# First overflow tile of a mixture-of-experts stage as a conditional 17th expert, without the barriers around it

## The reference, cut to what matters

```python
def moe(x, router_w, router_bias, w_gate, w_up, w_down):
    scores = sigmoid(x @ router_w)
    ...
    gate = take_along_axis(scores, idx, axis=-1)
    gate = gate / gate.sum(-1, keepdims=True)
    w = (one_hot(idx, N_EXPERTS) * gate[..., None]).sum(1)
    hg = einsum('nd,edf->nef', x, w_gate)
    hu = einsum('nd,edf->nef', x, w_up)
    hh = silu(hg) * hu * w[:, :, None]
    return einsum('nef,efd->nd', hh, w_down)

def trunk(...):
    for l in range(2):
        y, st = mixer_block(x, ...)
        x = layer_norm(ALPHA * x + y, ln1_g[l], ln1_b[l])
        x = layer_norm(ALPHA * x + moe(x, ...), ln2_g[l], ln2_b[l])
```

## Time and profile before

| what | value |
|---|---|
| median of 3 runs | 1659.1 us (1656.07 to 1663.48) |
| profiled execution, its own time | 1656.69 us |
| its span, first to last instruction | 1654.9 us |
| busy, share of the span | PE 1379.6 us (83%), PEld 892.5 us (54%), DVE 698.6 us (42%), ACT 440.1 us (27%), POOL 126.9 us (8%) |
| mean granted TensorE clock | 0.915 of full speed |
| HBM traffic | 187.48 MB read, 31.83 MB written, 133 GB/s over the span |

### The profile page before, as it was taken

The page is one execution under the profiler, slowest core; times in us unless marked ns, Lnnn a source line. Parts: engine busy times, 40 slices in busy tenths (PEclk is TensorE's granted clock), DMA queues, the critical chain, the costliest instruction groups (busy, mean ns, idle before and its releaser), DMA issues.

```text
span 1654.9 us, 19434 instructions
## 1 busy us (share of the span) xinstructions
PE 1379.6 (83%) x7575; PEld 892.5 (54%) x7575; DVE 698.6 (42%) x1381; ACT 440.1 (27%) x949; POOL 126.9 (8%) x157
## 2 busy tenths in 40 slices
PE   1999999988898489998089999999889957999950
PEld 1776765566676334444067676556667743444420
DVE  3442476665312622222436137676541262322317
ACT  2231123654213211121023211365430231221210
POOL 0100002100000000000210000030100001000002
PEclk9998997999999699999589899799999978999985
DMA  8320020302160268997523012030317015999835
GB/s 282 70 65 26 14 52 22 99 34 95 70 211 1 89 215 296 346 325 236 194 38 84 26 26 39 21 113 1 128 65 241 1 59 168 351 333 332 276 116 174
DMA packets 190988, 220.73 MB, mean 133 GB/s; under 512 B 47992, under 2 KB 164168, under 8 KB 188712
## 3 DMA queue, kind: packets, MB, share of 16 engines
q1 hardware_dynamic: 173800, 152.25, 30.5%
q0 software_dynamic: 12336, 49.82, 8.6%
q10 hardware_dynamic: 4752, 17.30, 2.6%
HBM read 187.48 MB, written 31.83 MB: 133 GB/s over the span
## 4 chain that ended last, share of the span: by engine, by line
PE 64%; DMA 14%; DVE 8%; issue 6%; ACT 3%; SPq 2%; DVEq 1%; ACTq 1%; POOL 1%; POOLq 0%; PEldq 0%
PE ps L524 15%; DMA over<-in_moe_w_up 10%; PE ps L1031 8%; PE ps L960 8%; PE ps L480 6%; PE ps L1047 3%; SPq L2220 2%; PE ps L799 2%; PE ps L581 2%; DMA y_rows<-over 1%; PE ps L917 1%; PE ps L841 1%; DVE zT L2085 1%; PE ps L494 1%; PE ps L484 1%
## 5 line engine op out<-in xcount | busy, mean ns | idle before, releaser
L1112 ACT ACTIVATE over<-ps 128x512 f32<-128x512 f32 (+11 forms) x390 | 186.5, 508 | 433.5 <-PE ps L524 151.7
L1031 PE MATMUL ps<-over 128*128 128x512 f32 x512 | 237.3, 618 | 28.1 <-DMA over<-in_moe_w_up 26.3
L524 PE MATMUL ps<-xT,wslot 128*128 128x296 f32 x960 | 252.9, 422 | 0.0
L524 PEld LDWEIGHTS ps<-xT,wslot 128*128 128x128 f32 x960 | 183.8, 194 | 57.4 <-issue 4.9
L480 PE MATMUL ps<-const,over 128*128 128x128 f32 (+4 forms) x984 | 149.6, 284 | 54.1 <-DVEq L1457 10.5
L1031 PEld LDWEIGHTS ps<-over 128*128 128x128 f32 x512 | 98.6, 198 | 146.6 <-issue 116.0
L480 PEld LDWEIGHTS ps<-const,over 128*128 128x128 f32 (+4 forms) x984 | 115.8, 142 | 103.2 <-issue 45.7
L2045 DVE TENSOR_SCALAR over<-over 128x256 f32<-128x256 f32 x33 | 9.7, 294 | 295.7 <-ACT over L1404 270.9
L1461 DVE COPY over<-ps 128x512 f32<-128x512 f32 (+5 forms) x134 | 68.6, 522 | 122.0 <-PE ps L524 65.8
L1047 PE MATMUL ps<-over 128*128 128x512 f32 x256 | 115.3, 593 | 1.2 <-DVE over L1461 1.2
L960 PE MATMUL ps<-mix,over 128*128 128x296 f32 x320 | 83.1, 413 | 0.0
(11 more groups left out here) (384 smaller groups left out, 1811.3 us busy)
## 6 DMA issues: line engine op xcount, KB each, us to landing
over<-in_moe_w_gate SPq DMA_DIRECT2D x33, 1024.0 KB, 9.8
over<-in_moe_w_up SPq DMA_DIRECT2D x33, 1024.0 KB, 12.2
over<-in_moe_w_down SPq DMA_DIRECT2D x33, 1024.0 KB, 6.4
y_rows<-over ACTq DMA_DIRECT2D x33, 512.0 KB, 7.3
wslot<-in_w_in SPq DMA_DIRECT2D x30, 512.0 KB, 4.4
over<-in_w_out SPq DMA_DIRECT2D x10, 512.0 KB, 7.0
y_rows<-over SPq DMA_DIRECT2D x1, 4608.0 KB, 13.5
x_rows<-zT SPq DMA_DIRECT2D x2, 2048.0 KB, 7.0
```

What stands on the lines that cost most here:

```text
L524: i = mm(b[:, 0:HALF], wslot[:, j % NSLOT, k, :], xT[:, k, SH[h]], start=(k == 0), stop=(k == KD - 1))
L1031: i = mm(b, xgT[:, e % 2, k, :], wgu[:, e % 2, k, :], start=(k == 0), stop=(k == KD - 1))
L1112: rel(f_(dst, src, ACT.Copy), key, "A")
```

## The change

It does three things.

- The zeros for the overflow tiles of `y_rows` are no longer issued by SP at the start, nor awaited there. ACT issues them in layer 0 as two DMAs of half the columns, after it has copied chunk 4 of the projection, from `lnr`, of which POOL has cleared 512 columns; they are awaited by ACT before it uses `lnr`, and by POOL before it gathers.
- The first overflow tile becomes step E = 16 of the pipeline: its groups are always taken, released and counted, its work stands in conditionals on the number of tiles, which each engine now loads ahead of the pipeline. SP may ask for its gate and up weights once expert 14's `up` is filled, and for its down weights once expert 14's `down` is.
- Both barriers around the overflow go. Overflow tiles 1 to 8 stay nested conditionals behind the pipeline. POOL waits for what it gathers: the writes of the overflow tiles that there are, the zeros, and the writes of the 16 tiles.

```diff
@@ PE @@
+                wait("overflow_known", l + 1)
+                count = pe.value_load(dyn[0:1, NOVER:NOVER + 1], min_val=0, max_val=NOVER)
+                def first_over(keys):
+                    pe.drain().then_inc(filled, len(keys))
+                def turn_first_over():
+                    b = [group(("xg", l, E, x), "A") for x in range(2)]
+                    with pe.If(count > 0):
+                        pe.wait_ge(S(f"over_fetched_{l}"), 16)
+                        for c in range(KD):
+                            tr(b[c // 4][:, (c % 4) * P:(c % 4 + 1) * P], xg[:, 1, c * P:(c + 1) * P], P)
+                    first_over(b)
+                def up_first_over():
+                    for x in range(2):
+                        drained(("xg", l, E, x))
+                    b = group(("up", l, E), "D")
+                    with pe.If(count > 0):
+                        pe.wait_ge(S(f"over_wgu_{l}"), 32)
+                        for c in range(KD):
+                            mm(b, xgT[:, 0, c, :], wgu[:, 0, c, :], start=(c == 0), stop=(c == KD - 1))
+                    first_over([b])
+                def down_first_over():
+                    wait("h_done", (l + 1) * (E + 1))
+                    b = group(("hT", l, E), "D")
+                    with pe.If(count > 0):
...
+                    first_over([b])
+                    drained(("hT", l, E))
+                    b = [group(("dn", l, E, x), "A") for x in range(2)]
+                    with pe.If(count > 0):
+                        pe.wait_ge(S(f"over_wdn_{l}"), 16)
...
+                    first_over(b)
                 turn(0)
                 for e in range(E + 1):
                     if e >= 1:
                         turn_h(e - 1)
                     if e < E:
                         up(e)
+                    else:
+                        up_first_over()
                     if e + 1 < E:
                         turn(e + 1)
+                    elif e + 1 == E:
+                        turn_first_over()
                     if e >= 1:
                         down(e - 1)
-                barrier(pe, "pe")
+                down_first_over()
+                drained(("up", l, E))
+                drained(("dn", l, E, 1))
...
-                overflow(0, pe.value_load(dyn[0:1, NOVER:NOVER + 1], min_val=0, max_val=NOVER))
-                barrier(pe, "pe")
+                overflow(1)
@@ ACT @@
                 projected(4)
+                if l == 0:
+                    act.wait_ge(S("vec_zeroed"), 1)
+                    for x in range(2):
+                        act.dma_start(y_rows[E * P:NTILE * P, x * (D // 2):(x + 1) * (D // 2)].rearrange("(i p) d -> p i d", p=P),
+                                      lnr[:, 0:D // 2].unsqueeze(1).to_broadcast([P, NOVER, D // 2])).then_inc(S("rows_cleared"), 16)
...
+                def gate_exp_first_over():
+                    full(act, ("up", l, E))
+                    act.wait_ge(S("h_done"), l * (E + 1) + E - 1)
+                    with act.If(count > 0):
+                        f_(eh[:, 0, :], bank(("up", l, E))[:, 0:F], ACT.Exp, scale=-1.0)
+                    act.drain().then_inc(S("hg_exp"), 1)
+                def y_out_first_over():
+                    for x in range(2):
+                        full(act, ("dn", l, E, x))
+                    act.wait_ge(S("y_written0"), 16 * (E // 2) * (l + 1))
+                    with act.If(count > 0):
...
+                        act.dma_start(y_rows[E * P:(E + 1) * P, :], yt[:, 0, :]).then_inc(S(f"over_written_{l}"), 16)
+                    act.drain().then_inc(rel_sem["A"], 2)
...
-                for q in range(2):
-                    act.wait_ge(S(f"y_written{q}"), 16 * (E // 2) * (l + 1))
-                barrier(act, "act")
+                y_out_first_over()
@@ DVE @@
+                hidden_first_over()
+                h_turned_first_over()
@@ POOL @@
-            g.memset(over[:, 0:D], 0.0)
+            g.memset(lnr[:, 0:D // 2], 0.0)
...
-                barrier(pool, "pool")
+                pool.wait_ge(filled, index[("xg", l, E, 1)] + 1)
...
+                        pool.wait_ge(S(f"over_written_{l}"), 16 * (k + 1))
+                overflow(0)
+                pool.wait_ge(S("rows_cleared"), 32)
+                for q in range(2):
+                    pool.wait_ge(S(f"y_written{q}"), 16 * (E // 2) * (l + 1))
@@ SP @@
-            ld(y_rows[E * P:NTILE * P, :].rearrange("(i p) d -> p i d", p=P), over[:, 0:D].unsqueeze(1).to_broadcast([P, NOVER, D]), "rows_cleared")
-            sp.wait_ge(S("rows_cleared"), 16)
...
                 with sp.If(count > 0):
-                    sp.wait_ge(filled, index[("dn", l, E - 2, 1)] + 1)
+                    sp.wait_ge(filled, index[("up", l, E - 2)] + 1)
                     load_overflow(0)
-                barrier(sp, "sp")
+                sp.wait_ge(filled, index[("dn", l, E, 1)] + 1)
```

More of the change, by code:

```diff
@@ L1414, in y_out, with x_in_first_over @@
                     act.dma_start(y_rows[e * P:(e + 1) * P, :], yt[:, e % 2, :]).then_inc(S(f"y_written{e % 2}"), 16)
+                def x_in_first_over():
+                    for x in range(2):
+                        full(act, ("xg", l, E, x))
+                    with act.If(count > 0):
+                        for x in range(2):
+                            f_(xgT[:, 0, 4 * x:4 * x + 4, :], bank(("xg", l, E, x)).rearrange("p (k n) -> p k n", k=4), ACT.Copy)
+                    act.drain().then_inc(rel_sem["A"], 2)
[6 more added lines that the diff above has]
+                def y_out_first_over():
+                    for x in range(2):
+                        full(act, ("dn", l, E, x))
+                    act.wait_ge(S("y_written0"), 16 * (E // 2) * (l + 1))
+                    with act.If(count > 0):
+                        for x in range(2):
+                            f_(yt[:, 0, x * 512:(x + 1) * 512], bank(("dn", l, E, x)), ACT.Copy)
+                        act.drain().then_inc(S(f"over_y_{l}"), 1)
+                        act.wait_ge(S(f"over_y_{l}"), 1)
+                        act.dma_start(y_rows[E * P:(E + 1) * P, :], yt[:, 0, :]).then_inc(S(f"over_written_{l}"), 16)
+                    act.drain().then_inc(rel_sem["A"], 2)
+                act.wait_ge(S("overflow_known"), l + 1)
+                count = act.value_load(dyn[0:1, NOVER:NOVER + 1], min_val=0, max_val=NOVER)
                 x_in(0)
@@ L2058, in hidden, with hidden_first_over, h_turned_first_over @@
                     sig("h_done")
+                def hidden_first_over():
+                    dve.wait_ge(S("hg_exp"), (l + 1) * (E + 1))
+                    b = bank(("up", l, E))
+                    with dve.If(count > 0):
+                        gated(eh[:, 0, :], b[:, 0:F], b[:, F:2 * F], hh[:, 0, :])
+                    dve.drain().then_inc(rel_sem["D"], 1)
+                    sig("h_done")
+                def h_turned_first_over():
+                    full(dve, ("hT", l, E))
+                    with dve.If(count > 0):
+                        v.tensor_copy(hT[:, 0, :, :], bank(("hT", l, E))[:, 0:2 * P].rearrange("p (f n) -> p f n", f=2))
+                    dve.drain().then_inc(rel_sem["D"], 1)
+                dve.wait_ge(S("overflow_known"), l + 1)
+                count = dve.value_load(dyn[0:1, NOVER:NOVER + 1], min_val=0, max_val=NOVER)
                 for e in range(E + 1):
```

85 lines of the change are left out of this document (46 added, 39 removed).

## The result

The changed kernel takes **1629.84 us** (median of 6 runs, 1622.96 to 1644.84) against 1660.35 for the kernel before in the same runs (6 runs, 1656.07 to 1665.0): ratio 0.9838, 95% interval 0.9806 to 0.9871. The forecast of 1627.5 us and its range hold. Run again later (5 runs), the same kernel gave 1626.56 (ratio 0.9793, 0.9766 to 0.9819). The profiled execution took 1624.2 us, with a span of 1622.4 against 1654.9.

A forecast was written before the change was run, and what follows sets the result against it. PE was 64% of the chain and DMA 14%; only places where PE stands still could shrink. 6.85 + 3.0 + 4.0 + 16.8 = 30.7 off the profiled 1656.69 gives 1626.0, set at 1627.5 us for run scatter; range 1620 to 1640.

The forecast's parts named there:

- Zeros leave SP's queue: Start of layer 0: first barrier waits for ACT, not the zeros; PE starts at 32.85 instead of 39.69, -6.85 us.
- Clock: Layer 0's first 64 products: with short PE idle time they take 16.21 us instead of 19.21, -3.0 (bounds 0 and -3.0).
- Zeros on ACT: Projection of layer 0: 4.6 MB issued on ACT's queue is covered by idle time, cost 0; uncovered, up to 13.5 us.
- Count loads: Ahead of the pipeline on PE, ACT and DVE: all wait for gathered rows, cost 0; uncovered, at most 0.43 us each.
- Conditionals: Pipeline steps of the overflow tile: each conditional with its drain costs 0.25 us; ten counted, 2.5 us.
- Layer 0's end: Last write to POOL's first gather in layer 0: gather at 794.73 instead of 798.75, -4.0 us (bounds -4.5 to 0).
- Layer 1's end: Overflow tile joins layer 1's pipeline: gather at 1595.75 instead of 1612.56, -16.8 us (bounds -18.8 to -12.4).
- the rest of the skip on engines that wait anyway: Both layers' ends: what is left of the overflow skip runs while engines await gathered rows, no extra cost.
- Clock or chunk loads: Rival: clock still falls at the start (+3.0) or gathers wait for chunk loads (+4.0), 1630.5 to 1631.5 us; chance 0.08.
- Late weights: Rival: the overflow tile's weights in layer 1 come 7 us later than worked out, 1634.5 us; chance 0.05.
- Zeros not hidden: Rival: the zeros delay the projection by 13.5 us, giving 1641 us; chance 0.05.
- Every conditional an instruction fetch: Rival: twelve new conditionals on the paths cost 3.40 us each, 1665.8 us; slower from 2.8 each; chance 0.05.

The follow-up runs named there:

- the kernel with the filler: The kernel before, with nine matmuls of 512 fp32 columns into an unread bank ahead of PE's first barrier: 1656.18 us (0.999).
- the eight more skips: The changed kernel with eight more never-taken conditionals, each with eight transposes, on PE ahead of down(14): one run, 1632.92 us.
- the kernel with late weights: The changed kernel, with SP asking for the overflow tile's gate and up weights only once expert 14's down product is filled: 1641.39 us (0.988).
- the pipeline alone: The changed kernel with the zeros back on SP's queue and awaited ahead of SP's first barrier: 1635.74 us (0.9846).
- the zeros last: The changed kernel with both halves of the zeros issued by SP as its last loads before the first barrier, not awaited there: 1629.22 us (0.9823).
- the two without further tiles: The changed kernel without steps for second and further overflow tiles: 1629.48 us (0.979); also with SP's chunk loads held until the last write landed: 1629.23 (0.9811).
- the skip of 320 transposes: The changed kernel with one more never-taken conditional on PE ahead of down(14), its body 320 transposes: one run, 1630.7 us.

## Why the prediction was right, step by step

- **Zeros leave SP's queue**, -6.85: measured -6.34 (first product 39.69 to 33.35), since ACT ended at 33.26 and not 32.63. **Clock**, -3.0: measured -3.00, and shown to be the clock by the kernel with the filler. Of the 9.44 us, 8.06 arrive at the first gather of tokens. The reason in the prediction, that SP's wait held the barrier, is shown by the zeros put last on SP's queue without it; but they did not have to leave that queue.
- **Zeros on ACT**, 0: right, by the 5.00 us of cover. **Count loads**, 0: nothing on the chain speaks against it.
- **Conditionals**, 0.25 each: near what PE's sequencer takes to jump over one step (0.20 to 0.25 us), but too high for the path. In layer 0 the two cost 0.04, not 0.5; in layer 1 the write is issued 22.61 us after up(15)'s end (1574.91 - 1552.30) where the prediction's steps give 23.76 (1592.85 - 1569.09). Of these 1.15 us, 0.4 lie ahead of the tile's up product, which began when its weights came, and 0.7 behind it. The step that failed is that each stands on the path: on PE a skip passes while the product ahead of it still runs, as the eight more skips show. What the rows do show is what the conditionals and drains on PE, ACT and DVE add together: from the end of the tile's up product to its hidden turn are 4.08 us (1568.66 - 1564.58) against 3.68 in the earlier trace rows. By the Trainium skill, "Advanced Engine Details and Errata", Control Flow Timing, a compare-and-branch takes about 108 ns. Here the branch took 0.03 to 0.07 us on ACT and DVE, 0.07 to 0.08 on PE where the step was entered, and 0.20 to 0.25 on PE where one step was skipped; these, not the page's figure, price a branch in this kernel.
- **Layer 0's end**, -4.0 to the gather: the mechanism is right, the size is off. The gather came 13.82 us after up(15) (783.80 - 769.98) against 16.56, that is -2.74. The terms that failed are the landing, taken as 2.61 from the earlier trace rows, which was 3.80 (+1.19), and POOL's 0.3, which was 0.85 (+0.55); the conditionals gave 0.46 back. The gain to PE's next work, 3.46, is larger than at the gather; unforeseen, 1.28 us of table load left the path there, against 0.74 lost between gather and first sum (7.28 for 6.54).
- **Layer 1's end**, -16.8: measured -16.99 (43.47 to 26.48), but by two errors that cancel: 1.15 us less up to the write's issue, 0.96 more from the write's issue to the gather (3.87 against 2.61 + 0.3). The weights were there in time: issued at 1547.13, landed 10.27 us later, 5.10 us after up(15)'s end, as PE was ready. Worked out were 5.6 us (1574.7 - 1569.09). What the prediction put at nothing, the rest of the skip on engines that wait anyway, was not nothing: it took back 1.72 us of the 16.99 before DVE's first sum (6.20 against 4.48), and its fetches slowed the writes.
- **Sum**: 30.7 forecast; 32.5 between the two profiled spans, 30.5 between the medians (33.9 with the repeat's). The 4.15 us from the experts of layer 0 in this execution are scatter, and without them the spans would lie 28.35 apart; that the sum comes so near is in part luck.
- **The rivals.** Clock or chunk loads: the clock kept its 3.00; chunk loads do slow the write, by part of 1.2 us. Late weights: what the kernel with late weights makes of it, 13 us, more than the 7 allowed; as built, they come just in time, and in four other profiles of the same pipeline (the pipeline alone, the zeros last, and the two without further tiles) PE waited 0.35 to 0.97 us for them. Zeros not hidden: no. Every conditional an instruction fetch: no short skip cost anything like 2.8 us. The trace of the kernel before could have said so for every engine but PE: its 3.40 us are PE's alone, and the branches over the same nine tiles' steps on ACT (L1429), DVE (L2069), POOL (L2199) and SP (L2364) took 0.03 to 0.07 us. On PE the skip of 320 transposes took 4.61 and 6.55 us, with fetches of instructions beside it, and 1.35 were seen where it was bare. That agrees with the rule of the Trainium skill, "Runtime: NRT & Kernel Launch", Instruction fetch mechanics, that a taken branch to a target outside the pages held must fetch first.

**Still open:** why POOL needs 0.71 us from its last wait to the gather (0.72 in layer 0 also with the write at 2.61; 0.15 to 0.26 where a barrier stands ahead of it); how the 3.80 us, with both beside the write, divide between them; and what makes the expert stage take 201 us in one execution and 212 in another.

## What to carry to other kernels

Read who releases a barrier: a transfer that nobody needs for 700 us kept PE idle for 8.12 us, where 1.14 were enough, and cost 3 more through the clock; issuing it last and dropping the wait was enough, without another queue. A conditional in a pipeline is cheap where it jumps over one step and the engine's sequencer reaches it while work is still in flight; look at each engine's own branches in the trace before pricing them. Merging a lone tail stage pays mostly through loads that can be asked for earlier (13 of 17 us here). When a barrier goes, look at what used to run between the two: skips, fetches and next-stage loads now lie beside the last write.

## What was not expected of the hardware

- A 512 KB write that lands in 2.61 us alone took 3.45 and 3.50 with four instruction fetches of 0.04 MB beside it, 2.81 to 3.15 with one (layer 1 in eight of the profiles), and 4.23 with loads issued 0.1 us ahead of it.
- Of SP's loads behind the zeros, the second was held 9.54 us when the zeros were one DMA; when they were two halves at the end, the next issues, already behind the barrier, took 9.23 for five.
- An idle time of 10.17 us in front of a product cost 2.9 us more in the product itself (10.01 against 7.13), as at the start, where 8.12 us of idle time cost 3.00.
- PE's jumps took 0.20 to 0.25 us over one step, 4.61 and 6.55 over 320 transposes, 3.40 and 3.61 over the steps of nine and of eight overflow tiles before and 5.38 and 4.32 over eight after; on ACT, DVE, POOL and SP the branches over the nine tiles' steps took 0.03 to 0.07.
